# The order of VectorE's steps in two transformer mixers, changed in seven places

## The reference

```python
h = x + 0.5 * swiglu(rms_norm(x, norm_ffn1[i]), w_ffn1_in[i], w_ffn1_out[i])
u = rms_norm(h, norm_mix[i])
q, k, v, c, g = jnp.split(u @ w_in[i], splits, axis=-1)      # 512, 128, 128, 1024, 2048 columns
y_attn = window_attention(norm(q), norm(k), v, sink[i], rel_bias) @ w_attn_out[i]   # 8 heads, 2 for k and v
c = silu(layer_norm(depthwise_conv(c_val * sigmoid(c_gate))))                      # 31 taps, 512 channels
y_conv = c @ w_conv_out[i]
g_attn, g_conv = jnp.split(jax.nn.sigmoid(g), 2, axis=-1)
h = h + (g_attn * y_attn + g_conv * y_conv) @ w_o[i]
h = h + 0.5 * swiglu(rms_norm(h, norm_ffn2[i]), w_ffn2_in[i], w_ffn2_out[i])
x = h + (p[i] @ w_pe_proj[i]) * jax.nn.sigmoid(rms_norm(h, norm_pe[i]) @ w_pe_gate[i])
```

```python
proj = rmsnorm(x, ln1_g[layer]) @ w_in[layer]
qa, ka, va, cq, ckv, kr, qc, kc, vc = jnp.split(proj, split_idx, axis=-1)
out_a = mixer_dilated(rope(qa), rope(ka), va)                # 6 heads of 64, keys at strides 1, 4, 16
out_b = mixer_mla(cq, ckv, kr, ...)                          # 6 heads, q = norm(cq) @ w_uq, k and v = norm(ckv) @ w_ukv
out_c = mixer_diff(qc, kc, vc, ...)                          # 4 heads, difference of two softmaxes, then a norm
x = x + jnp.concatenate([out_a, out_b, out_c], axis=-1) @ w_o[layer]
x = x + jnp.square(jax.nn.relu(rmsnorm(x, ln2_g[layer]) @ w_up[layer])) @ w_down[layer]
```

## Time and profile before

| | |
|---|---|
| time, median of 3 runs | 1790.14 us (1789.99 to 1790.19) |
| the profiled execution's own time | 1790.14 us |
| its span, first to last instruction | 1788.3 us |
| PE busy | 1775.1 us (99%), 11422 matmuls |
| DVE busy | 1105.5 us (62%) |
| ACT busy | 893.1 us (50%) |
| DMA | 303 MB, 170 GB/s on average |

### The profile page before, as it was taken

The page is one execution under the profiler, slowest core; times in us unless marked ns, Lnnn a source line. Parts: engine busy times, 40 slices in busy tenths (PEclk is TensorE's granted clock), DMA queues, the critical chain, the costliest instruction groups (busy, mean ns, idle before and its releaser), DMA issues.

```text
span 1788.3 us, 28974 instructions
## 1 busy us (share of the span) xinstructions
PE 1775.1 (99%) x11422; PEld 1616.9 (90%) x11422; DVE 1105.5 (62%) x1604; ACT 893.1 (50%) x1304; POOL 26.5 (1%) x32
## 2 busy tenths in 40 slices
PE   9999999999999999999999999999999999999998
PEld 9998898899988999888889998889898988989896
DVE  6554588765555655468776554667565556756554
ACT  5444456544444544355654443567553446745342
POOL 0000000000000000000000000000000000000000
PEclk9999999999999999999999999999999999999999
DMA  8854533554455555543345545534355543435541
GB/s 303 225 185 166 211 113 123 189 176 184 177 176 189 189 188 177 199 166 118 134 173 195 178 168 185 183 131 144 115 189 200 177 163 117 143 115 191 199 178 48
DMA packets 45852, 303.22 MB, mean 170 GB/s; under 512 B 5104, under 2 KB 6256, under 8 KB 12312
## 3 DMA queue, kind: packets, MB, share of 16 engines
q1 hardware_dynamic: 45720, 301.36, 47.8%
HBM read 300.02 MB, written 1.31 MB: 168 GB/s over the span
## 4 chain that ended last, share of the span: by engine, by line
PE 97%; ACT 1%; DVE 1%; issue 1%; POOLq 0%; POOL 0%; ACTq 0%; DVEq 0%
PE ps L469 15%; PE ps L471 15%; PE ps L470 15%; PE ps L520 14%; PE ps L521 14%; PE ps L522 14%; PE ps L542 2%; PE ps L798 2%; PE ps L616 1%; PE ps L822 1%; PE ps L627 1%; PE ps L649 1%; PE ps L807 1%; PE ps L497 0%; PE ps L495 0%
## 5 line engine op out<-in xcount | busy, mean ns | idle before, releaser
L1512 DVE TENSOR_TENSOR wlo<-raw,whi 128x1024 fp32r<-128x1024 f32 (+4 forms) x388 | 657.1, 1705 | 415.7 <-ACT whi L1001 415.5
L1001 ACT ACTIVATE whi<-raw 128x1024 fp32r<-128x1024 f32 (+4 forms) x388 | 554.2, 1443 | 356.3 <-PE ps L471 223.8
L520 PE MATMUL ps<-x_hi,wlo 128*128 128x256 f32 x2048 | 582.1, 284 | 1.4 <-DVE wlo L1512 1.4
L521 PE MATMUL ps<-x_lo,whi 128*128 128x256 f32 x2048 | 579.5, 283 | 0.0
L522 PE MATMUL ps<-x_hi,whi 128*128 128x256 f32 x2048 | 579.5, 283 | 0.0
L520 PEld LDWEIGHTS ps<-x_hi,wlo 128*128 128x128 f32 x2048 | 393.0, 192 | 3.1 <-DVE wlo L1512 1.6
L521 PEld LDWEIGHTS ps<-x_lo,whi 128*128 128x128 f32 x2048 | 393.0, 192 | 0.5
L522 PEld LDWEIGHTS ps<-x_hi,whi 128*128 128x128 f32 x2048 | 393.0, 192 | 0.0
L469 PE MATMUL ps<-whi,hid_hi 128*128 128x512 f32 x600 | 233.9, 390 | 0.0
L470 PE MATMUL ps<-wlo,hid_hi 128*128 128x512 f32 x600 | 233.5, 389 | 0.0
L471 PE MATMUL ps<-whi,hid_lo 128*128 128x512 f32 x600 | 233.4, 389 | 0.0
(11 more groups left out here) (265 smaller groups left out, 1497.8 us busy)
## 6 DMA issues: line engine op xcount, KB each, us to landing
raw<-in_w SPq DMA_DIRECT2D x261, 1024.0 KB, 4.8
raw<-in_w SPq DMA_DIRECT2D x12, 768.0 KB, 4.2
raw<-in_w SPq DMA_DIRECT2D x14, 512.0 KB, 3.3
raw<-in_w SPq DMA_DIRECT2D x4, 576.0 KB, 3.5
raw<-in_w SPq DMA_DIRECT2D x4, 432.0 KB, 3.2
bias<-line_scratch SPq DMA_DIRECT2D x8, 192.0 KB, 10.1
h<-in_x SPq DMA_DIRECT2D x2, 512.0 KB, 5.7
out<-h SPq DMA_DIRECT2D x2, 512.0 KB, 2.7
```

Source lines behind the costliest of these rows:

```text
L520: e.matmul(o, wl, x_hi[:, c, :], start=first and n == 0 and m % 2 == 0, stop=False)
L521: e.matmul(o, wh, x_lo[:, c, :], start=False, stop=False)
L1001: e.activation(w_at(whi, j, off, n), raw[:, j % RAW, off:off + n], ACT.Copy).then_inc(s_hi, count)
L1512: e.tensor_tensor(w_at(wlo, j, off, n), raw[:, j % RAW, off:off + n], f32(w_at(whi, j, off, n)), ALU.subtract).then_inc(s_lo, count)
```

## The change

PE's and DVE's programs are written in another order in seven places; ACT's in one; no instruction is added or dropped, and no buffer or size changes.

1. First mixer, DVE: the four small instructions (two memsets of `kT`, two of the pad, a scale of `q_norm`) come first in `mixer1`, and `spread` comes after `use(q[0])` instead of ahead of everything.
2. First mixer, DVE: the gate pieces use `use` instead of `behind`.
3. First mixer, DVE: the sums of `w_conv_out` come in pairs behind both halves of `wlo`, instead of between them.
4. Second mixer: `qa` is prepared at step 11 of the chain instead of 12 (all engines), and DVE's rope of the second half of `qa` comes behind the low parts of the next piece.
5. Second mixer, DVE: `k_[1]` goes through `behind`, `sub_norm` comes between the two ropes of k, and `x_of_mix` behind the chain's step. PE transposes `mix` chunks 6 and 7 between the two `va` pieces instead of in the middle of the first, and ACT takes them out after it.
6. Second mixer, DVE: in `chain` the closing comes after the new scores.

```diff
 MAP_AT = [None] * 2 + list(range(8)) + [None] * 5 + list(range(8, 20)) + [None] * 3
-PREP_STEP = {0: "kc", 1: "qc", 12: "qa", 13: "kb", 14: "qb", 19: "ka"}
+PREP_STEP = {0: "kc", 1: "qc", 11: "qa", 13: "kb", 14: "qb", 19: "ka"}
 CLOSING = {3: ("c", 768, 4), 7: ("c", 896, 4), 11: ("b", 384, 4), 13: ("b", 640, 2), 17: ("a", 0, 4), 19: ("a", 256, 2)}
...
     out_frees(8, "k")
-    def first_turns():
-        e.wait_ge(s_c, 2 * l + 2)
-        transposes(("wo2", l, 6), mix, (6, 7), [(s_xlo, xv("wo2", l, 7))])
-    simple(va_[0], X, need, bks[9], True, False, mid=first_turns)
+    simple(va_[0], X, need, bks[9], True, False)
+    e.wait_ge(s_c, 2 * l + 2)
+    transposes(("wo2", l, 6), mix, (6, 7), [(s_xlo, xv("wo2", l, 7))])
     simple(va_[1], X, need, bks[9], False, True)
...
     tick()
-    use(va_[0], mid=lambda: x_of_mix(l, 6, 2))
+    use(va_[0])
+    x_of_mix(l, 6, 2)
     use(va_[1], end=False)
...
 def mixer1(l, nxt):
+    for s in range(2):
+        e.memset(kT[64 - 64 * s:128 - 64 * s, s, :], 0.0).then_inc(s_kz, 1)
+    e.memset(pad[:, :, 0:15], 0.0).then_inc(s_pad0, 1)
+    e.memset(pad[:, :, 271:286], 0.0).then_inc(s_pad0, 1)
+    e.tensor_scalar(sm[:, 0:1], k("q_norm", l), -0.125, None, ALU.mult, ALU.bypass).then_inc(s_qg, 1)
     c0, c1 = pair_specs(l, (768, 1024), (1280, 1536)), pair_specs(l, (1024, 1280), (1536, 1792))
...
     q, kv_ = halves("w_in", l, (0, 512)), piece("w_in", l, LO + HI, (512, 768))
-    spread("mix", l)
     use(c0[0])
...
     use(q[0])
-    for s in range(2):
-        e.memset(kT[64 - 64 * s:128 - 64 * s, s, :], 0.0).then_inc(s_kz, 1)
-    e.memset(pad[:, :, 0:15], 0.0).then_inc(s_pad0, 1)
-    e.memset(pad[:, :, 271:286], 0.0).then_inc(s_pad0, 1)
-    e.tensor_scalar(sm[:, 0:1], k("q_norm", l), -0.125, None, ALU.mult, ALU.bypass).then_inc(s_qg, 1)
+    spread("mix", l)
     use(c0[1])
...
         u = halves("w_in", l, (1792 + 512 * g, 2304 + 512 * g))
-        behind(u[0])
-        behind(u[1])
+        use(u[0])
+        use(u[1])
     drain(att)
...
-    def summed(g, t, spec, bk):
-        ga, gc = (thg[:, i, t, g * 512:g * 512 + 512] for i in range(2))
-        if t == 0:
-            e.wait_ge(s_row0, ROWS0[spec])
-        else:
-            e.wait_ge(s_used, NUM[spec] + 1)
-        e.wait_ge(s_g, 8 * l + 4 + 2 * g + t + 1)
-        e.scalar_tensor_tensor(out=gc, in0=gc, scalar=1.0, in1=BANKS[bk][t][:, :], op0=ALU.add, op1=ALU.mult).then_inc(s_cm, 1)
-        e.wait_ge(s_hm, 4 * l + 2 * g + t + 1)
-        e.wait_ge(s_cm, 4 * l + 2 * g + t + 1)
-        e.tensor_tensor(ga, ga, gc, ALU.add).then_inc(s_m, 1)
-    p, q = (piece("w_conv_out", l, LO, cols(g)) for g in range(2))
-    summed(0, 0, p, "SO")
-    low(NUM[p] + AHEAD, True)
-    summed(0, 1, p, "SO")
-    summed(1, 0, q, bank("mix", l, 10))
-    sum_turns(0)
-    low(NUM[p] + AHEAD)
-    summed(1, 1, q, bank("mix", l, 10))
-    low(NUM[q] + AHEAD)
+    for g in range(2):
+        spec = piece("w_conv_out", l, LO, cols(g))
+        bk = "SO" if g == 0 else bank("mix", l, 10)
+        use(spec, mid=(lambda: sum_turns(0)) if g == 1 else None)
+        for t in range(2):
+            ga, gc = (thg[:, i, t, g * 512:g * 512 + 512] for i in range(2))
+            if t == 0:
+                e.wait_ge(s_row0, ROWS0[spec])
+            else:
+                e.wait_ge(s_used, NUM[spec] + 1)
+            e.wait_ge(s_g, 8 * l + 4 + 2 * g + t + 1)
+            e.scalar_tensor_tensor(out=gc, in0=gc, scalar=1.0, in1=BANKS[bk][t][:, :], op0=ALU.add, op1=ALU.mult).then_inc(s_cm, 1)
+            e.wait_ge(s_hm, 4 * l + 2 * g + t + 1)
+            e.wait_ge(s_cm, 4 * l + 2 * g + t + 1)
+            e.tensor_tensor(ga, ga, gc, ALU.add).then_inc(s_m, 1)
     a, b = halves("w_o", l, cols(0)), halves("w_o", l, cols(1))
...
             turn2(l, at[i - 2])
+        if at[i] is not None:
+            scores2(l, at[i])
         if i >= 3 and at[i - 3] in CLOSING:
             closed(l, at[i - 3])
-        if at[i] is not None:
-            scores2(l, at[i])
         yield
...
     uq = [piece("mla_w_uq_2", l, (0, 1, 2), cols(g, 288)) for g in range(2)]
+    tick()
+    low(NUM[uq[0]] + AHEAD, True)
     rope(l, "q", qa[:, 0, :], 6, 64, 0, 32, 0, out2(l, "q", 0))
     tick()
-    low(NUM[uq[0]] + AHEAD, True)
+    low(NUM[uq[0]] + AHEAD)
+    tick()
+    low(NUM[uq[1]] + AHEAD, True)
     rope(l, "q", qa[:, 1, :], 6, 64, 0, 32, 1, out2(l, "q", 1))
     tick()
-    low(NUM[uq[0]] + AHEAD)
-    behind(uq[1])
+    low(NUM[uq[1]] + AHEAD)
     for t in range(2):
...
     sub_sums(l)
-    tick()
-    low(NUM[k_[1]] + AHEAD, True)
+    behind(k_[1])
+    rope(l, "k", ka[:, 0, :], 6, 64, 0, 32, 0, out2(l, "k", 0))
+    tick()
+    low(NUM[va_[0]] + AHEAD, True)
     sub_norm(l)
-    tick()
-    low(NUM[k_[1]] + AHEAD)
-    rope(l, "k", ka[:, 0, :], 6, 64, 0, 32, 0, out2(l, "k", 0))
-    tick()
-    low(NUM[va_[0]] + AHEAD, True)
     rope(l, "k", ka[:, 1, :], 6, 64, 0, 32, 1, out2(l, "k", 1))
+    tick()
...
     x_of_mix(6, 2)
-    tick()
     low(NUM[va_[0]] + AHEAD)
```

More of the change, by code:

```diff
@@ L2090, in mixer2 @@
                 sub_sums(l)
-                tick()
-                low(NUM[k_[1]] + AHEAD, True)
-                sub_norm(l)
-                tick()
-                low(NUM[k_[1]] + AHEAD)
+                behind(k_[1])
                 rope(l, "k", ka[:, 0, :], 6, 64, 0, 32, 0, out2(l, "k", 0))
@@ L2098, in mixer2 @@
                 low(NUM[va_[0]] + AHEAD, True)
+                sub_norm(l)
                 rope(l, "k", ka[:, 1, :], 6, 64, 0, 32, 1, out2(l, "k", 1))
+                tick()
                 def x_of_mix(c, n):
```

## The result

The changed kernel takes 1805.12 us (median of 4 runs, 1803.58 to 1805.49) against 1790.16 us before (4 runs): 15.0 us more, a ratio of 1.0082 with the interval [1.0064, 1.0099]. The forecast of slower was right; the size was not: 1798.7 was forecast, and 1805.12 lies above the range, which ended at 1803.0. The profiled execution took 1803.1 us, 1801.3 of it span.

The account below looks back on a forecast made before the run. PE, busy 1775.07 of 1788.30 us, was taken as the bound, so only its holes could grow. Six terms, 0.6 + 1.0 + 0.85 + 0 + 1.65 + 0.2, gave 4.3 us a layer, 8.6 in all: 1798.7 us, range 1792.5 to 1803.

Parts of the forecast that it names:

- step 4: Second mixer, `qa` prepared earlier: product 1.66 us late, less 0.58 and 1.04 given back; net taken as 0 a layer.
- Rival D: Holes of 1.6 us make PE's clock fall to 1.2 GHz: +16 us for four holes, 1814 us; 2 in 100.
- step 5: Second mixer, `sub_norm` and `x_of_mix` moved: PE's scores wait for DVE's copy out of their PSUM bank, 1.65 us a layer.
- The bound: Whole kernel: time is PE's work plus its holes; only holes grow, matmul busy time stays near 1775 us.
- Steps 1 and 3: First mixer, a layer: `spread` later, PE waits 0.6 us for `dg`; `w_conv_out` sums later, PE's transposes wait 0.85 us.
- Step 2: First mixer's gates, `use` for `behind`: a DVE-ACT loop of 4.35 us delivers `qs` late, PE waits 1.0 us a layer.
- step 6: Second mixer, closing behind the score: one of four closings on a path, at 1253.05, costs 0.2 us a layer.
- A: Second mixer: moved transposes pay, waits for `qkc` and `tmp` go, `qa` is in time: 1789.8 us; 10 in 100.
- B: DVE-ACT loops catch up within some laps: 1795.3 us, or 1793.0 if wholly; 22 in 100.
- C: Each DVE step takes its full busy time and the `qkc` gain doesn't come: 6.4 us a layer, 1802.9; 8 in 100.

Follow-up runs that it names:

- no_qa: The changed kernel with part 4 undone (`qa` prepared at step 12 of the chain, rope early): 1802.87 us, ratio 1.0065.
- no_mixk: The changed kernel with part 5 undone (`sub_norm`, `x_of_mix` and the `mix` transposes in their old order): 1798.61 us, ratio 1.0044.
- qa_only: The kernel before with part 4 alone (`qa` prepared at step 11, rope of its second half later): 1790.81 us, ratio 0.9999.
- mixk_hi_first: The kernel before with part 5 alone, and ACT's `x_of_mix` (`c_hi`) ahead of the exponentials: 1791.65 us, ratio 1.0003.
- xmix_only: The kernel before with, of part 5, only DVE's `x_of_mix` moved behind the chain's step: 1790.59 us, ratio 1.0003.
- closing_only: The kernel before with part 6 alone (closing behind the new scores in DVE's chain): 1790.39 us, ratio 0.9997.
- after: The changed kernel itself, all six parts against the kernel before: median 1805.12 us; its profile is of an execution of 1803.1 us.
- mixk_only: The kernel before with part 5 alone (`sub_norm`, `x_of_mix` and the `mix` transposes moved): 1795.22 us, ratio 1.0023.
- hole_mid: The kernel before with `spread` later and two extra DVE memsets of `kT` ahead of it: 1793.3 us, ratio 1.0016.
- hole_dense: The kernel before with `spread` later and four extra DVE memsets of `kT` ahead of it: 1795.96 us, ratio 1.003.
- subnorm_only: The kernel before with, of part 5, only `sub_norm` moved between the ropes of k: 1801.46 us, ratio 1.0062.
- after_hi_first: The changed kernel with ACT's `x_of_mix` (`c_hi`) moved ahead of the background step's exponentials: 1799.16 us, ratio 1.0046.

## Why the prediction was wrong in size

The forecast was +8.6 us, the measured change is +15.0. Of the 6.4 between them 3.2 are two falls of the granted clock, which the sum put at nothing, 1.4 are step 4, 1.4 the other holes, and 0.4 stay open. The holes alone, 11.4, would give 1801.5, inside the range; the falls put the time outside it.

- **Rival D is the step that failed.** The clock's fall was left out of the sum and given 2 in 100, because four idle stretches of 0.8 us in before had left the clock at 1.00. From 0.8 us nothing follows for 1.6. (Before also has 1.42 us at its start at 1.00, which the prediction didn't use, and which would have misled in the same way.) In its place the runs show the clock at 0.50 behind the hole of step 5, at 1.6 us a fall: in one layer of the changed kernel's profile, in both of `no_qa`'s, and none in `no_mixk`, which is 6.5 us faster with 3.5 us fewer holes. The price in D was wrong too, 16 us for four holes; that a fall doubles the time for some 4 us behind it and so costs 4 us was in no row of before. The count of two falls in the median execution is reckoned from times, not seen.
- **The bound.** PE's work plus its holes: right, and all the new waits are the ones named. "Matmul busy time stays near 1775" failed: it is 1780.1. The slower matmuls of the fall are 1.6 of these 5.0 us; the rest is overlap of neighbours that the holes break.
- **Steps 1 and 3** were sized low, 0.6 for 0.82 and 0.85 for 1.07 a layer. The chain of step 1 was right to 0.2 us (`dg` was computed to start at 212.21 and did at 212.39; the small instructions ahead of it are five, not four). What the sum left out is that a hole costs up to 0.2 us more than PE's idle time. Idle time counts from the end of the last matmul, but without a hole the next one starts before that end (a product of 384 columns takes 0.33 us, and they start every 0.17). So 0.67 idle at `dg` moved PE by 0.84.
- **Step 2**, 1.0 for 1.08: right. The loop ran at 4.33 us a lap (score at 280.86, then 285.19) for 4.35 computed.
- **Step 4**, 0 for 0.7: the failed sentence is "Net 1.66 - 0.58 - 1.04 = 0.04". Its first term held: measured from the offset at which the second mixer comes to this place, 6.03, the product behind the `qa` transposes is 7.74 - 6.03 = 1.71 us late for 1.66. So did the last: the `qkc` wait gave back 1.0. But of the 0.58 us at the transposes' old place only some 0.15 came back, since PE now waits 0.30 us for `vb` there (the row at 1226.71). The gain at ACT's `tmp` and step 6's new wait, neither of which the prediction had, cancel in part and only lengthen the wait for `qa`, whose end is set by DVE. In `qa_only`, without step 6's order, the product is 0.4 us less late, and the part alone costs 0.2 to 0.3.
- **Step 5**, 1.65 for 1.73: size and path were right. The rows have the path as computed: DVE's score at 1247.38 behind sub_norm, exponentials at 1248.05, `c_hi` at 1248.94, `c_lo` at 1249.65. Its cause is ACT's order: with `c_hi` ahead of the exponentials neither sub_norm nor DVE's own reorder costs anything (`mixk_hi_first`), and with ACT's old order DVE's reorder alone doesn't (`xmix_only`). How much of the 1.73 is sub_norm's 0.67 no run separates.
- **Step 6**, 0.2 for 0.3: right for the closing at 1253.05; the gain of 0.87 and the wait of 0.4 at another closing, which `closing_only` shows, were not seen at all, as only one of the closings was called "on a path".

A and B did not happen: `qa` was not in time, and nothing caught up. C's 1802.9 is the nearest of the forecasts to the measured time, but by luck: DVE's steps kept their overlap (1.14 us from the `wlo` at 279.72 to the score at 280.86), the `qkc` gain did come, and C has no fall of the clock.

## What to carry to other kernels

On an engine that takes its work in order, ask for each moved instruction not only what it waits for, but what stands ahead of it in the queue of the engine that feeds it: one activation behind two exponentials was worth 6 us. When a matrix engine that is 99% busy gets a new hole, price it at its idle time plus some 0.2 us, and above a microsecond give the clock's fall a term of its own, with a chance: in these runs neither the size of a hole nor its place alone told whether the clock fell. Parts of a change that remove the same wait don't add. And work that moves away may have hidden a wait at its old place, as the `qa` transposes hid that for `vb`.

## What the runs showed of the hardware

The granted clock of PE fell to 0.50 behind 1.25 us of idle time that followed 0.36 us and some short transposes in three of the six cases that the profiles have (`after`, `no_qa`, `mixk_only`), for 3 to 4 us, at a cost of some 1.6 us. A single hole of 1.43 us at `qa` left it at 1.00 in six of six. Holes of 1.33 and 1.23 us (`hole_mid`) and of 2.09 and 2.01 us (`hole_dense`) did so in their profiles; by their times, other executions of `hole_dense` may have had falls. One of 3.33 us made it fall in both layers of `subnorm_only`, once for some 7 us. At the start of a kernel, first waits of 2.61 and 2.08 us did it (`mixk_hi_first`, `after_hi_first`), and waits of 1.42 to 1.87 us in 14 profiles did not. So two executions of one program can differ by 1.5 us or a multiple, which makes a median of a few runs of such a kernel uncertain by as much.
